# Multiplying the first two modulation pieces ahead of a layer's barrier, and fetching the first input tiles there

## What is computed

```
c_act = silu(c)
for l in range(2):
    mod = c_act @ w_ada[l] + b_ada[l]            # 1024 x 6144 matrix: twelve pieces of 512 columns
    shift1, scale1, gate1, shift2, scale2, gate2 = split(mod, 6)
    h = rms_norm(x, norm1_g[l]) * (1 + scale1) + shift1
    proj = h @ w_in[l]                           # 1024 x 1472
    ... attention and convolution on proj, output matrix
    x = x + gate1 * mix
    h2 = rms_norm(x, norm2_g[l]) * (1 + scale2) + shift2
    x = x + gate2 * expert_choice_ffn(h2, ...)   # 16 experts, 64 tokens each
```

## Time and profile before

| | |
|---|---|
| median of three executions | 2645.95 us |
| the profiled execution | 2650.9 us |
| its span in the trace | 2649.2 us |
| PE busy | 2484.0 us (94%) |
| DVE, ACT, POOL busy | 1109.6, 871.3, 294.7 us |
| start of layer 0 and of layer 1 on PE (L534) | 27.75 us, 824.08 us |
| first input matmul of layer 0 and of layer 1 (L567) | 46.84 us, 842.45 us |

### The profile page before, as it was taken

The page is one execution under the profiler, slowest core; times in us unless marked ns, Lnnn a source line. Parts: engine busy times, 40 slices in busy tenths (PEclk is TensorE's granted clock), DMA queues, the critical chain, the costliest instruction groups (busy, mean ns, idle before and its releaser), DMA issues. The chain is left out here.

```text
span 2649.2 us, 31866 instructions
## 1 busy us (share of the span) xinstructions
PE 2484.0 (94%) x12913; PEld 1487.9 (56%) x12913; DVE 1109.6 (42%) x1700; ACT 871.3 (33%) x1195; POOL 294.7 (11%) x126
## 2 busy tenths in 40 slices
PE   6989799999997989799999998999999999989998
PEld 5834533333335834533333337887788777756665
DVE  4974322222223974322222225647521112456765
ACT  4246111111114247111111116556532234245553
POOL 0002000000000002000000005000244423200000
PEclk8988899999998988899999999999999999989999
DMA  9700579999999600589999996532223321159995
GB/s 339 275 1 37 221 307 409 410 410 410 410 409 346 244 1 34 221 321 409 410 410 410 410 409 191 168 93 81 79 75 97 131 71 57 48 177 373 358 354 208
DMA packets 276596, 650.49 MB, mean 246 GB/s; under 512 B 12144, under 2 KB 110718, under 8 KB 276222
## 3 DMA queue, kind: packets, MB, share of 16 engines
q1 hardware_dynamic: 273310, 638.87, 64.2%
q0 software_dynamic: 2592, 7.87, 0.8%
q10 hardware_dynamic: 576, 2.10, 0.2%
HBM read 641.99 MB, written 8.39 MB: 246 GB/s over the span
## 5 line engine op out<-in xcount | busy, mean ns | idle before, releaser
L829 PE MATMUL ps<-ring,scr 128*64 128x512 f32 x1952 | 425.3, 593 | 0.8 <-DMA ring<-in_w_up 0.8
L829 PEld LDWEIGHTS ps<-ring,scr 128*64 128x64 f32 x1952 | 138.7, 137 | 277.2 <-issue 274.0
L851 PE MATMUL ps<-ring,scr 128*64 128x512 f32 x1024 | 231.9, 606 | 1.4 <-ACT scr L1047 1.4
L1579 POOL TENSOR_TENSOR raw_r<-raw,w_high 128x2048 fp32r<-128x2048 f32 (+1 forms) x38 | 165.3, 4359 | 460.0 <-ACT w_high L1846 460.0
L1601 PE MATMUL ps<-x_high,w_high 128*128 128x512 f32 x464 | 186.6, 402 | 5.4 <-DVE y L2242 5.4
L1603 PE MATMUL ps<-x_high,raw_r 128*128 128x512 f32 x464 | 184.3, 397 | 0.0
L1602 PE MATMUL ps<-xT_r,w_high 128*128 128x512 f32 x464 | 182.9, 394 | 0.0
L1123 DVE SCALAR_TENSOR_TENSOR one_hot_T<-h_tok,convw,one_hot_T 128x512 f32<-128x512 f32 x240 | 170.5, 763 | 1.8
L497 POOL TENSOR_TENSOR one_hot_T_r<-hy,one_hot_T_r 128x1024 fp32r<-128x1024 f32 x16 | 38.5, 2405 | 1124.0 <-ACT one_hot_T_r L1059 1124.0
L1331 DVE TENSOR_TENSOR scr<-scr,ps 128x512 f32<-128x512 f32 x32 | 22.0, 688 | 312.5 <-PE ps L829 312.5
L2720 DVE TENSOR_TENSOR ring_r<-ring,ring_high 128x2048 fp32r<-128x2048 f32 x56 | 127.6, 2286 | 58.4 <-ACT ring_high L2598 57.9
(11 more groups left out here) (563 smaller groups left out, 4536.2 us busy)
## 6 DMA issues: line engine op xcount, KB each, us to landing
ring<-in_w_down SPq DMA_DIRECT2D x64, 2048.0 KB, 15.2
ring<-in_w_up SPq DMA_DIRECT2D x62, 2048.0 KB, 18.4
ring<-in_w_gate SPq DMA_DIRECT2D x60, 2048.0 KB, 14.9
ring<-in_w_up SPq DMA_DIRECT2D x56, 1024.0 KB, 7.2
ring<-in_w_ada SPq DMA_DIRECT2D x22, 2048.0 KB, 13.2
ring<-in_w_down SPq DMA_DIRECT2D x28, 1024.0 KB, 7.7
raw<-in_w_in SPq DMA_DIRECT2D x24, 1024.0 KB, 5.1
raw<-in_w_in SPq DMA_DIRECT2D x20, 512.0 KB, 5.3
```

Of the source, the lines that this page charges most:

```text
L829: mm = pe.matmul(ps[CAP * half:CAP * (half + 1), 1 + j // 2, :], x_e[:, at_x:at_x + CAP], weights[:, k, half * HALF:(half + 1) * HALF], st ...
L851: mm = pe.matmul(ps[CAP * half:CAP * (half + 1), 4, :], hidT[:, at_f:at_f + CAP], weights[:, k, half * HALF:(half + 1) * HALF], start=(j = ...
L1579: pool.tensor_tensor(dst, src, high.bitcast(F32), ALU.subtract).then_inc(w_ready, 1)
```

## The change

Pieces 0 and 1 of the modulation are multiplied by a new function `ada_ahead` in the block before: for layer 0 at the end of PE's stream in the prologue, for layer 1 after the last expert's matmuls and before the last scatter. The results wait in bank 7, columns 0 to 255. For that the spread `c` is made in another place as well, by DVE. In the layer only the pieces 2 and 3 are left ahead of the input matmuls; the spread root goes to bank 3 behind piece 2, and piece 3 follows. `ada_used` counts two less, and the pieces 4 and 5 are loaded without a wait. `load_input` moves from the layer's start into the prologue, ahead of the store of the tables, and into the tail of layer 0, behind the modulation loads and a wait until all of the last expert's weights are used.

```diff
+ADA_PRE = 2
+def ada_ahead(pe, M, c):
+    for kt in range(KT):
+        for g in range(4):
+            pe.matmul(M["ps"][GROUP * g:GROUP * (g + 1), 7, c * P:(c + 1) * P], c_spread_ahead(M)[:, kt, :], ada_place(M, ADA_PLACES[c])[:, kt, g * P:(g + 1) * P],
+                      start=(kt == 0), stop=(kt == KT - 1))
 # prologue, sync
             for c in range(4):
                 load_ada(sp, A, M, 0, c, ahead)
+            load_input(sp, A, M, 0, ahead)
             sp.wait_ge(p_act, 2)
             sp.dma_start(A["rope"], tables).then_inc(ahead["tables"], 16)
 # prologue, tensor
+            pe.wait_ge(x_kept, KT)
+            pe.wait_ge(p_spread, 1)
+            for c in range(ADA_PRE):
+                pe.wait_ge(ahead["ada"][c], 16)
+                ada_ahead(pe, M, c)
 # prologue, vector
+            dve.wait_ge(c_act, 1)
+            dve.tensor_copy(c_spread_ahead(M), M["c_col"][:].unsqueeze(2).to_broadcast([P, KT, GROUP])).then_inc(p_spread, 1)
 # layer, sync
             def ada_chunk(c):
                 before = max(b for b in range(c) if ADA_PLACES[b] == ADA_PLACES[c])
-                sp.wait_ge(ada_used, before + 1)
+                if before >= ADA_PRE:
+                    sp.wait_ge(ada_used, before - ADA_PRE + 1)
-            load_input(sp, A, M, l, ahead)
             ada_chunk(4)
...
                 load_ada(sp, A, M, after, 3, ahead)
+                sp.wait_ge(chunk_used, 6 * EXPERTS)
+                load_input(sp, A, M, after, ahead)
 # layer, tensor
             pe.wait_ge(c_spread, 1)
-            ada_chunk(0, 0)
+            ada_chunk(2, 2)
             pe.wait_ge(n_inv, 1)
             pe.wait_ge(vec_ready, 2)
-            broadcast(7, root).then_inc(n_bc, 1)
-            for c in range(1, 4):
-                ada_chunk(c, c)
+            broadcast(3, root).then_inc(n_bc, 1)
+            ada_chunk(3, 1)
...
+            with pe.If(l < DEPTH - 1):
+                pe.wait_ge(st_free, EXPERTS + 1)
+                pe.wait_ge(c_again, 1)
+                for c in range(ADA_PRE):
+                    pe.wait_ge(ada_in[ADA_PLACES[c]], ada_landed(c, l + 1))
+                    ada_ahead(pe, M, c)
 # layer, scalar
-            for c in range(3):
-                ada_kept(c, c)
+            for c in range(ADA_PRE):
+                ada_kept(c, 7, c * P)
             for i in range(2):
                 w_in_split_tile(i)
-            ada_kept(3, 3)
+            ada_kept(2, 2)
+            ada_kept(3, 1)
 # layer, vector
-                dve.tensor_tensor(hT[:, kt, :], xT[:, kt, :], ps[:, 7, :], ALU.mult).then_inc(n_xn, 1)
+                dve.tensor_tensor(hT[:, kt, :], xT[:, kt, :], ps[:, 3, :], ALU.mult).then_inc(n_xn, 1)
...
+            with dve.If(l < DEPTH - 1):
+                dve.tensor_copy(c_spread_ahead(M), M["c_col"][:].unsqueeze(2).to_broadcast([P, KT, GROUP])).then_inc(c_again, 1)
```

More of the change, by code:

```diff
@@ L112, in ada_landed, with c_spread_ahead @@
     return 16 * ADA_PLACES.count(place) * n + 16 * (ADA_PLACES[:c].count(place) + 1)
+ADA_PRE = 2
+def c_spread_ahead(M):
+    return M["one_hot_T"][:, EXPERTS * S - MT * D:EXPERTS * S - MT * D + KT * GROUP].rearrange("p (k n) -> p k n", k=KT)
+def ada_ahead(pe, M, c):
[3 more added lines that the diff above has]
+                      start=(kt == 0), stop=(kt == KT - 1))
 def vector_rows(M):
@@ L203, in prologue @@
         sem(n) for n in ("x_turned", "c_turned", "x_kept", "c_act", "ones_set"))
-    angle_ready, p_step, p_act, p_sq = sem("angle_ready"), sem("p_step"), sem("p_act"), sem("p_sq")
+    angle_ready, p_step, p_act, p_sq, p_spread = (sem(n) for n in ("angle_ready", "p_step", "p_act", "p_sq", "p_spread"))
     sq = M["hy"][:, KT * S:2 * KT * S].rearrange("p (k n) -> p k n", k=KT)
@@ L390, in layer @@
     ye_hi_ready, ye_lo_ready, out_done, x2_ready = (sem(n) for n in ("ye_hi_ready", "ye_lo_ready", "out_done", "x2_ready"))
-    d_step, t_sq = sem("d_step"), sem("t_sq")
+    d_step, t_sq, c_again = sem("d_step"), sem("t_sq"), sem("c_again")
     mem_in, mem_step, mem_var, mem_root, mem_norm, mem_mm, mem_vec, memT_ready, memT_split, kv_split = (
@@ L428, in _ @@
                     ada_chunk(c)
-            sp.wait_ge(ada_used, 12)
+            sp.wait_ge(ada_used, 12 - ADA_PRE)
             sp.dma_start(w_uq, at("w_uq").rearrange("a (k p) n -> p (a k) n", p=P)).then_inc(uq_in, 16)
@@ L483, in _ @@
         def _(pool):
-            pool.wait_ge(ada_used, 4)
+            pool.wait_ge(ada_used, 4 - ADA_PRE)
             pool.memset(w_r[:, :, EXPERTS:GROUP], 0.0)
@@ L534, in _ @@
             pe.transpose(ps[:, 5, 0:NVEC], rowsA[0:NVEC, :], ident[0:NVEC, 0:NVEC]).then_inc(rowsT_done, 1)
-            pe.transpose(ps[:, 7, 0:TAPS * CT], rowsB[0:TAPS * CT, :], ident[0:TAPS * CT, 0:TAPS * CT]).then_inc(rowsT_done, 1)
+            pe.transpose(ps[:, 4, 0:TAPS * CT], rowsB[0:TAPS * CT, :], ident[0:TAPS * CT, 0:TAPS * CT]).then_inc(rowsT_done, 1)
             def ada_chunk(c, bank):
@@ L903, in _, with ada_kept @@
             act.activation(root, ps[:, SQ_SUM, 0:P], ACT.Sqrt, bias=eps, scale=1.0 / D).then_inc(n_root, 1)
-            def ada_kept(c, bank):
-                act.wait_ge(ada_used, c + 1)
+            def ada_kept(c, bank, col=0):
+                if c >= ADA_PRE:
+                    act.wait_ge(ada_used, c - ADA_PRE + 1)
                 if c >= 4:
                     act.wait_ge(ada_cols, c - 3)
-                act.activation(ada_row[c % 4], ps[:, bank, 0:P], ACT.Copy).then_inc(ada_rows, 1)
+                act.activation(ada_row[c % 4], ps[:, bank, col:col + P], ACT.Copy).then_inc(ada_rows, 1)
             def w_in_split_tile(at_tile):
@@ L1092, in _ @@
             dve.wait_ge(rowsT_done, 2)
-            dve.tensor_copy(convw[:], ps[:, 7, 0:TAPS * CT]).then_inc(vec_ready, 1)
+            dve.tensor_copy(convw[:], ps[:, 4, 0:TAPS * CT]).then_inc(vec_ready, 1)
             dve.tensor_copy(c_rep, M["c_col"][:].unsqueeze(2).to_broadcast([P, KT, GROUP])).then_inc(c_spread, 1)
```

## The result

| | before | change |
|---|---|---|
| median, same chip and session | 2645.07 us (4 runs, 2641.8 to 2647.7) | 2663.76 us (4 runs, 2661.0 to 2669.4) |
| ratio, 95% interval | | 1.0064 [1.0041, 1.0087] |
| the profiled execution | 2650.9 us | 2661.7 us |
| its span | 2649.2 us | 2659.9 us |

The change made the kernel slower, as forecast, by more than forecast: 2656 was said, with 2661 as the upper end. The spans differ by 10.7 us, and they can be taken apart. (The numbers of lines are higher after: L534 is L560 now, L541 is L567, the first input matmul L567 is L592, the loads L141 and L147 are L157 and L163, the last sum L513 is L539.)

What follows compares the result with a forecast made beforehand. Compute engines were taken to pace the layer body, SP's issuing the prologue's end. Layer 0 +9.1 and layer 1 +0.8 give +9.9 us, 2660.8 for the profiled execution, 2656 for the median; range 2651 to 2661, 8 in 10 2647 to 2661.

Steps and rivals of the forecast that it cites:

- Layer 0's barrier: Prologue: SP, held issuing tiles and store until 40.0, moves L534 from 27.75 to 40.8, +13.0 us (+11.3 to +13.7).
- From there to the input matmuls: L534 to L567: DVE's order sets the modulation; 15.2 us in layer 0 (-3.9), 14.7 in layer 1 (-3.7).
- Nothing swallows it: Layer body after L567: paced by compute engines, so a layer start's loss or gain goes one for one to the end.
- The prologue hides the pieces: Prologue: pieces 0 and 1 cost 7.3 us of PE, done by 29.1 while PE waits until 40: free.
- The tail: End of layer 0: SP, through its tiles at 823.4, sets the barrier; L534 of layer 1 at 828.6, +4.5 us.
- the +6.5 bound: Tail of layer 0, upper bound: code fetch behind the jump slowed by the full queue, another 2 us.
- rival 4: Code fetch behind full queues costs 2 us at both starts and the jump in layer 1; about 2660, chance 0.13.
- The end of layer 1: PE's jump over the two pieces falls into 3.5 us of idle time: 0, at most 1.7 us.
- the term from the profiled execution down to the median of three: The median of three runs lies 4.95 us below the profiled execution, so 2660.8 became 2655.9.
- Rival (1): Prologue: the queue takes the four tiles without holding SP, the barrier stays; -6.3 us in all, 2639.7, chance 0.08.
- (2): Layer 0's loss at L567 is swallowed by a stage waiting for transfers, +9.1 shrinks below 5; about 2648, chance 0.08.
- Rival (3): Tail of layer 0: PE, not SP, sets the barrier; +9.1 + 1.3 - 3.7 = +6.7, 2652.7, chance 0.16.

Runs made afterwards that it cites:

- r3_tiles_ahead_only: The kernel before with only the input tiles' loads moved ahead, into prologue and tail; 2665.99 us, 1.0067 of the kernel before.
- r4_tail_tiles_only: The change with layer 0's tiles issued at the layer's start, layer 1's still in layer 0's tail; 2652.25 us, 1.0010 of the kernel before.
- r6_second_in_scatter: The change with piece 1 between the last scatter's matmuls and layer 0's tail under one condition; 2661.33 us, 1.0064 of the kernel before.
- r10_tiles_layer0_last: r6_second_in_scatter with PE's two conditional parts at the layer's end exchanged, layer 1's first; 2662.58 us, 1.0060 of the kernel before.
- r7_all_three: The change with tiles at the layer's start, piece 1 within the last scatter, copies of pieces 2 and 3 ahead of the splits; 2646.31 us, 0.9998.
- r9_layer0_last: r7_all_three with PE's two conditional parts at the layer's end exchanged, layer 1's first; 2645.89 us, 0.9983 of the kernel before.
- r2_tiles_at_start: The change with the input tiles issued at the layer's start again, only the two pieces ahead; 2649.43 us, 1.0000 of the kernel before.
- r5: r2_tiles_at_start with ACT's copies of pieces 2 and 3 ahead of the two tile splits; 2649.24 us, 1.0008 of the kernel before.
- r8_half_the_tiles: The change with tiles 0 and 1 loaded ahead, 2 and 3 at the layer's start; 2662.03 us, 1.0056 of the kernel before.

## Why the prediction was right in kind and wrong in size

**Layer 0's barrier: right.** The forecast had SP through at 40.0 and L534 at 40.8; they are at 39.50 and 40.27 (+12.52 for +13.0). The tiles were in at 37.76, and the store behind them took 1.69 us, near piece 4's 1.46. `r3_tiles_ahead_only` shows that the tiles alone do this, `r4_tail_tiles_only` that it goes without them.

**From there to the input matmuls: right.** 14.40 us for 15.2, and 14.55 for 14.7. DVE's order carries it, as said: the bias sum came right behind the eight tiles. Of the 0.8 us in layer 0, 0.7 are the spread root, 1.35 us for the 2.04 I had taken from layer 0 before; the clock rose in the middle of it, and piece 3 behind it took 1.95 us.

**Nothing swallows it: right.** The body from the first input matmul to the last expert's end is 757.39 us for 758.62. That 1.23 is less than the same stretch moves between two profiles of the change (757.39 and 754.64), and `r4_tail_tiles_only`, whose inputs start 7.8 us earlier, has 758.11.

**The prologue hides the pieces: right.** PE ended piece 1 at 28.8, 11 us ahead of the barrier.

**The tail: the step that failed.** Forecast +4.5 us, measured +7.98. It was said that SP, not PE, sets this barrier, by a hold of 16.3 us. The hold was 16.02, and where PE has no stop SP does set it (`r3`, `r6`, `r10`). In the change as it ran, PE set it: SP's next issue (834.92) comes 1.88 us behind PE's last sum, the step of the kernel before, and 3.86 us behind SP's own last issue, where it is 2.1 us if SP is last (`r6`, `r10`). Three terms were too small or missing:

- The hold began later. I took SP to be done with piece 3 at 807.14, 1.68 us behind the last expert's end. It was done 2.76 us behind it (814.82 against 812.06), and the tiles began at 2.98: +1.3 us. The loads of the pieces began at the same distance from the last expert's end (19.4 us ahead of it in both), but the first three held SP 16.85 us, not 15.79. `r3_tiles_ahead_only` has 16.92, so it is not the pieces on PE; what decides it was not found.
- From SP's end to the next layer's first matmul I took 5.15 us, from PE's idle time before. Where SP is last it is 6.0, 6.9 and 6.6 us (`r3`, `r6`, `r10`): +0.8 to +1.8. In the profile before, the 5.15 us ran from PE's own end, and what SP needs to reach the barrier was not in it.
- PE stopped inside the sums. I had named a slower code fetch, at 2 us, but behind the loop's jump (the +6.5 bound) and at both starts and in layer 1 (rival 4), not here. PE stopped for 4.68 us, ended at 833.04 instead of about 828.4, and so was later than SP (831.06). It is 5.62 us from there to L560. The tails with this stop are 25.73 to 27.89 us (four profiles), those without it 25.07 to 25.72 (three): it adds 0 to 2.8 us, about 1 in the profile above.

From the profile after the sum is: +1.3 for the later beginning, -0.3 for the hold (16.02 for 16.3), and +2.45 from SP's end to L560 (838.66 - 831.06 = 7.60 for 5.15), in which SP's own way to the barrier and the stop lie together. That is +3.45, and the tail missed by +7.98 - 4.5 = +3.48. With it the forecast's steps give +9.9 + 3.5 less what the other steps came out below the forecast (0.5, 0.8 and 0.1): +12.0; with the body's -1.2 it is the +10.7 of the profiles.

**The end of layer 1: right at the low end.** 0.0 us for 0 to 1.7. PE's idle time ahead of the last scatter there is 1.45 and 2.01 us, where it was 1.45 and 2.03.

**The range.** The sum of the forecast for the profiled execution was 2660.8 us, and it took 2661.7: the tail's +3.5 was for the most part made up by the other steps, and that is luck. What it missed was the median: 2663.76 for 2655.9. Of these 7.9 us, 0.9 are the sum's; 4.95 are the term from the profiled execution down to the median of three, which I took whole off the forecast; and the change's median lay 2.1 us above its profiled execution instead of below it. The kernel before alone ran from 2641.0 to 2659.3 us in 29 runs of one session, and the change from 2653.0 to 2671.6 in 12, so such a term is spread and not a property of the kernel, and the range had no room for it. The loss itself is 11 us by the session with more runs (1.0042) and 17 by the first (1.0064); the intervals overlap between 1.0041 and 1.0057, that is +11 to +15 us, and it isn't settled closer.

**What the stop in the sums is.** Transfers in windows of the profile after: first while PE stands (826.9 to 828.5 us), then 828.5 to 829.5:

```profile
q1 hardware_dynamic: 625, 0.56, 108.4%
...
q1 hardware_dynamic: 548, 0.29, 109.4%
q8 instruction: 1, 0.02, 7.6%
```

The columns are packets, MB and share. A queue of instructions moves one packet (0.02 MB) some 2 us after PE has run out at 826.87, among the packets of the tiles, and PE goes on at 831.54. The same in `r7_all_three`, 818 to 819 us, with no packet in the data queues:

```profile
q8 instruction: 1, 0.02, 5.5%
```

One such packet alone proves little: the kernel before moves them too, and the profile does not say for which engine. Their number behind PE's last sum, up to the next layer's first matmul, tells more. First `r7_all_three` (815.1 to 823.3), then `r9_layer0_last` (818.1 to 823.7) and the kernel before (818.9 to 824.1):

```profile
q8 instruction: 3, 0.05, 2.5%
...
q8 instruction: 2, 0.03, 2.7%
...
q8 instruction: 2, 0.03, 2.6%
```

Where the branch stands behind the sums there is one packet more, and it goes when the branch does. With the tiles ahead it is the same: three in `r6_second_in_scatter`, two in `r10_tiles_layer0_last`, though SP's barrier hides the time.

The stop is 1.13 us (`r2`) and 3.04 us (`r5`) with the tiles at the layer's start, and 4.41 to 4.95 us with the tiles in the queue (four profiles). It went behind the sums when the branch was moved there, and disappeared when the branch was moved into the hole (`r9`). So it belongs to the taken branch. That the traffic in the queue makes it longer is likely from these six profiles, but not shown: 1.13 and 3.04 us differ too, with the tiles at the layer's start in both. Rival (4) had the right cause, in a place that it did not name. The Trainium skill, page "Runtime: NRT & Kernel Launch", section "Instruction fetch mechanics", says that a taken branch to code outside the loaded pages forces a fetch of it before the engine can go on; the trace agrees, with that packet and a price of 1.1 to 5.0 us. In layer 1 and at both starts no such loss was seen, so (4) as a whole was wrong. Rival (1), the tiles taken by the queue without holding SP, is refuted by both SP rows; (2) by the body. Rival (3), PE setting the tail, came true only through the stop, and with a later barrier, not the earlier one it stood for; in `r6_second_in_scatter`, without the stop, PE is done 4.3 us ahead of SP.

PE's clock in two windows of the tail of the profile after, the scatter with the adds, and the rest of the sums (columns as in rows 1):

```profile
818.60:825.40 6.80, 6.48 (x84) 4.41 (x86) 4.14 (x7) 3.22 (x6) 0.00 (x0) 1.00 1.05 387
...
831.50:833.10 1.60, 1.50 (x21) 0.97 (x21) 0.00 (x0) 0.00 (x0) 0.00 (x0) 0.50 1.17 291
```

With the pieces in the hole the scatter ran at 1.00 where it had 0.50, and the adds took 5.36 us. Behind the stop the clock is down again: 21 sums take as long as 43 had. The forecast said that the faster scatter would change nothing, since SP comes later. With PE last that doesn't hold: in `r4_tail_tiles_only` and `r8_half_the_tiles` the clock over piece 1 and the scatter was 0.77 to 0.79, PE ended the sums 22.4 and 22.2 us behind the last expert where the two profiles of the change have 21.0 and 20.7, and the tails are 27.89 and 27.55 us, not 26.60 and 25.73.

## What to carry to other kernels

A load moved ahead of a barrier is not free because its engine is idle there: an issuing instruction holds its engine while much is in flight, and the barrier waits for that engine, so count how long the issues themselves take (16 us for four tiles of 512 KB behind four transfers of 2 MB here), and keep issues that nothing needs yet behind the barrier, where they cost only their own queue. Work that shortens a chain pays only down to the next thing in it, which here was the landing of those same tiles (1.3 us of 3.9) and a stop behind a branch; put the branch where the engine waits anyway. A forecast of some tenths of a per cent needs the spread of the kernel's own runs in its range, and the profiled execution compared with its own kind.

## What the runs showed of the hardware that I had not expected

- **The same code runs at different speeds in different executions.** The next rows are windows of 17 us in one place of layer 0's attention (columns as in rows 1). The profile before:

```profile
164.00:181.00 17.00, 17.00 (x31) 7.10 (x31) 7.80 (x15) 4.43 (x8) 0.00 (x0) 0.50 0.00 0
```

The profile after:

```profile
172.00:189.00 17.00, 17.00 (x31) 7.26 (x30) 7.67 (x15) 4.43 (x8) 0.00 (x0) 0.50 0.00 0
```

The change again:

```profile
172.00:189.00 17.00, 14.33 (x47) 5.82 (x46) 13.35 (x27) 7.88 (x16) 0.00 (x0) 1.00 0.00 0
```

The pieces ahead with the tiles at the start:

```profile
164.00:181.00 17.00, 15.62 (x48) 6.68 (x46) 11.52 (x23) 6.39 (x12) 0.00 (x0) 0.91 0.00 0
```

At a granted clock of 0.50 PE does 31 matmuls in it, at 1.00 47. From the first score matmul of the attention to the last of the output matrix, layer 0 takes 134.0 to 134.6 us in the seven profiles of twelve that have 17 us at 0.50 there, and 128.5 to 131.5 in the other five, in kernels that don't differ there; the change has both. PE was busy at a clock of 1.00 for over 110 us up to the fall. One profile against another can be 6 us off for this alone, and it may be a part of why the span of `r2_tiles_at_start` (2641.4) lies so far below its median (2649.43). What decides it was not found.
- **A stop behind a taken branch is 1.1 to 5.0 us long,** and it can stand 43 matmuls behind the branch. Barrier, clearing of the semaphores and jump back to the next layer together cost 5.0 to 5.6 us between PE's last and next matmul when PE is last.
- **The four tiles held SP 16.0 to 16.3 us wherever they stood** behind the modulation pieces (eleven holds in six profiles), 9.6 to 11.3 us at layer 0's start behind the store (six profiles), and 4.5 to 5.4 us at layer 1's start with the modulation pieces landed (five).
